# Tokens feature first from the host, the late chunk loaded later, VectorE scaling from PSUM

## The chip, the cores and the metric

The kernel runs on one core of one Trainium2 chip. The time is the device time in microseconds (us) of one execution; below it, "span" is the time from the first to the last instruction of a profiled execution. Engines: TensorE (PE, with its weight loads PEld), VectorE (DVE), ScalarE (ACT), GpSimd (POOL) and SyncE (SP), which here only issues DMAs.

## What is computed

A trunk of two layers over 1024 latent tokens and 256 context tokens, width 1024, in float32. Layer 0 is a chunked gMLP beside a bidirectional diagonal state space model (S5), layer 1 is grouped-query attention. The change lies wholly in the front of layer 0: modulation and row norm of the tokens, and the first products of `h` with `we_in`.

```python
def _ada(cond, w, b):
    m = jax.nn.silu(cond) @ w + b            # cond: c for latents, c_ctx for context
    return jnp.split(m, 3, axis=-1)          # shift, scale, gate

def _prologue(x, ctx, c, c_ctx, g, w_mod, b_mod):
    hx = _rms_norm(x, g) * (1 + sc[:, None]) + sh[:, None]
    hc = _rms_norm(ctx, g) * (1 + scc) + shc
    h = jnp.concatenate([hc, hx], axis=1)    # 1280 tokens x 1024 features

# layer 0
u, v, g_a, xs, g_b = jnp.split(h @ w_in, [...], axis=-1)
y_a = _chunk_gmlp(u, v, ...) * silu(g_a)     # layer norm of v, 128x128 mixing of tokens
y_b = _s5_bidir(xs, ...) * silu(g_b)         # scan over tokens, state operators from lam, dt, B, C
x = x + gt * (concat(y_a, y_b) @ w_out)
```

`_rms_norm` is `x * rsqrt(mean(x*x) + eps) * g`. The state operators of S5 (`exp` and `sin`/`cos` of `lam*dt`, powers up to 8, and their products with B and C) are computed in the kernel too.

## The kernel before

Tokens are cut into three chunks, `CHUNKS = [(0, 256), (256, 512), (768, 512)]`: the context, and two chunks of latents. Features are eight blocks of 128 (`KT`). Every large product is made of three TensorE products, of a rounded high part and a low part of each operand: `hi` and `h_lo` for the tokens (regions A and B), and the two halves of a weight slot for the weights. ScalarE rounds (`weights_round`, `h_round`), VectorE subtracts (`weights_rest`, `h_rest`). Weights come through a ring of three 2 MiB slots in an order written out by hand in `early` (L297); a slot is loaded again when the products of its last tenant are done.

The front, in order:

- SP (from L410) loads the column vectors, the five token pieces of 1 MiB each (context, then four of x, one token a row of 4 KB), modulation blocks 0 and 1, v(0), blocks 2 and 3 outside the ring, v(1), blocks 4 and 5, xs(0). ScalarE's queue (L651 to L657) loads the identity, `lam`, `log_dt`, and `braw`, `Cx` and `dT` (B, C and D of S5).
- ScalarE squares each token tile with a sum (L662), takes the root of all ten sums (L726), and scales the even tiles (L729); VectorE refines the root (`row_rstd`, L1024) and scales the odd tiles (L1112).
- TensorE makes modulation block m (`mods(m)`, 64 products of two rows) and turns its row into columns (`mod_cols`), and turns the scaled tokens feature first (`to_features(q)`, transposes into four PSUM banks). ScalarE (k = 0, 2, 3, 5, 6) and VectorE (k = 1, 4, 7) copy these out (`raw_evac`) into `hT0`.
- `half_evac(e)` on VectorE gathers scale and shift of feature half e. `h_round(e, q)` on ScalarE and `h_rest(e, q)` on VectorE make `hi` and `h_lo` of half e of chunk q. The first products of v need half 0 of chunk 0.
- v is made token by token (`v_part`): the first half of its columns for tiles 0 to 5 over k 0 to 3, then over k 4 to 7, then the second column half and the rest. Then come the 12 parts of xs (feature block x chunk; chunk 0 has 256 columns, the others 512). Between tiles and parts stand other jobs in the order of `after_v` and `after_xs` (L341, L343); TensorE and ScalarE both go by these two lists, each with its own part of a job.

Beside this, VectorE carries the parameters of S5: two exponentials (`exp_`, L1040), the sine, the parity of the quarter turns, a reciprocal, which releases `s_trig` (L1125). GpSimd waits for it (L540) and makes the cosine, the discretized lambda and its powers, some 60 small instructions, each waiting for the one before. VectorE waits for their end (L1151), then makes BB, the B operators (`build_bl(0)` to `(3)`) and the C operators (`build_cl(0)` and `(1)`, ended by a copy that releases `s_cl_ok`). The lists say who needs what:

```python
after_v = {1: [("mods", 4)], 2: [("cols", 4)], 5: [("mods", 5)], 6: [("cols", 5), ("xs", 0)], 7: [("bop", 0)], 8: [("bop", 4)],
           9: [("lags", 0)]}
after_xs = {0: [("xs", 1)], 2: [("bop", 8)], 4: [("ws", 0)], 5: [("lags", 1)], 6: [("gb", 0), ("bop", 12)], 7: [("vg", 0)],
            8: [("vg", 5)]}
```

`("xs", 1)` is ScalarE's rounding of xs(1). `("lags", half)` is on TensorE the lag products of S5 (`lags`, needs `s_cl_ok` half + 1), on ScalarE the copies of their result (`k_copies`), which VectorE's `k_diagonal(half)` waits for. `("bop", j)` are transposes of the B operators and their way out. SP stores the C operators with `cop_out(half)` (four DMAs, after `s_cl_ok`) and the lags with `kt_out(half)` (15 DMAs, after `k_diagonal`). On SP's queue stand, in this order: `cop_out(0)`, load of xs(1), `kt_out(0)`, load of gb(0), `cop_out(1)`, `kt_out(1)`, load of the B operators. When all xs parts are done, TensorE mixes v (L1798, ten tiles), and then multiplies by the B operators (L1814).

The helper lines of the rows: L1008 and L1011 are `tt` and `ts` of VectorE, L649 is `copy` of ScalarE, L1598 is `tr` of TensorE, L1613 is `mods`, L1732 to L1734 are `token_part`, L1743 to L1745 `feature_part`, L532 to L538 are GpSimd's small helpers, L403 is `ring_load`, L432 `cop_out`, L439 and L442 `kt_out`.

## Time and profile before

| | us |
|---|---|
| median of 3 runs | 1304.54 (1301.89 to 1306.85) |
| the profiled execution | 1301.15 |
| its span | 1299.3 |
| TensorE busy | 1223.0 (94%) |
| VectorE busy | 851.6 (66%) |
| ScalarE busy | 518.3 (40%) |
| GpSimd busy | 445.6 (34%) |

A share of busy time is an average over stages with different limits, and a busy TensorE may be waiting inside its pipeline. So the profile is read by stage: the timelines of the engines over the first 340 us, in which each group of instructions has its start, its length and, in brackets, how long its engine stood idle before it and who ended that. "DMA to landing" is the time from the start of the issue to the last byte.

### The profile page before, as it was taken

The page shows a single profiled execution, that of the slowest core. Times are in us where ns is not written, and L with a number is a line of the kernel's source. Part 1 is how long each engine was busy: PE and PEld are TensorE (multiplying, and loading weights), DVE is VectorE, ACT ScalarE, POOL GpSimd, SP SyncE. Part 2 cuts the span into 40 slices and gives each one's busy share as a digit, 9 for nine tenths or more (in the row PEclk, how much of TensorE's full clock was granted, in tenths as well). Part 3 has the DMA queues.
Part 4 walks back from the last instruction along what each step waited for, and adds up shares of the span by engine and source line. Part 5 has one row for each costly group of instructions (what it writes and reads, how often), then busy time and mean ns, then how long its engine had stood idle before and what let it go on. Part 6 is the DMA issues. An engine that isn't in the chain of part 4 may idle for free.

```text
span 1299.3 us, 21119 instructions
## 1 busy us (share of the span) xinstructions
PE 1223.0 (94%) x8508; PEld 1079.1 (83%) x8508; DVE 851.6 (66%) x1494; ACT 518.3 (40%) x956; POOL 445.6 (34%) x358
## 2 busy tenths in 40 slices
PE   1799989999999899999999999999999999999997
PEld 1789878888888848999999998877788888888997
DVE  6697956989925253136484899448877877776125
ACT  6632353320015331034524432146666666665012
POOL 0600000000000003332112212139999888988332
PEclk9899999999999999999999999999999999999999
DMA  9614677425422962103211112330000000000402
GB/s 347 241 66 130 153 209 247 148 81 203 162 90 85 324 231 56 64 33 116 70 44 34 33 66 81 111 100 9 9 17 9 17 9 17 17 9 9 162 28 103
DMA packets 87408, 127.99 MB, mean 99 GB/s; under 512 B 12912, under 2 KB 59376, under 8 KB 86512
## 3 DMA queue, kind: packets, MB, share of 16 engines
q1 hardware_dynamic: 77200, 110.81, 25.8%
q10 hardware_dynamic: 10112, 15.85, 3.5%
q8 instruction: 67, 1.10, 0.3%
q14 instruction: 29, 0.24, 0.1%
HBM read 95.71 MB, written 30.93 MB: 97 GB/s over the span
## 4 chain that ended last, share of the span: by engine, by line
PE 78%; DVE 11%; DMA 4%; ACT 3%; POOL 3%; issue 2%; SPq 0%; ACTq 0%; POOLq 0%; DVEq 0%
PE ps L1732 10%; PE ps L1734 10%; PE ps L1733 10%; PE ps L1743 5%; PE ps L1744 5%; PE ps L1745 5%; PE ps L1986 3%; DVE region_d L1008 3%; PE ps L2020 2%; PE ps L2021 2%; PE ps L2022 2%; PE ps L2006 2%; PE ps L2009 2%; PE ps L2008 2%; PE ps L2007 2%; PE ps L1598 2%
## 5 line engine op out<-in xcount | busy, mean ns | idle before, releaser
L1732 PE MATMUL ps<-w_hi,a_hi 128*128 128x256 f32 x896 | 256.6, 286 | 9.9 <-DVE b_lo L1109 6.3
L1733 PE MATMUL ps<-w_lo,a_hi 128*128 128x256 f32 x896 | 254.9, 284 | 0.0
L1734 PE MATMUL ps<-w_hi,c_lo 128*128 128x256 f32 x736 | 208.2, 283 | 0.0
L601 POOL TENSOR_TENSOR region_b<-region_b,region_d 128x256 f32<-128x256 f32 x40 | 29.7, 749 | 510.0 <-DVE region_d L1412 510.0
L1732 PEld LDWEIGHTS ps<-w_hi,a_hi 128*128 128x128 f32 x896 | 173.2, 193 | 12.2 <-issue 3.7
L1733 PEld LDWEIGHTS ps<-w_lo,a_hi 128*128 128x128 f32 x896 | 173.4, 194 | 0.0
L594 POOL TENSOR_TENSOR w_lo<-weight_ring,w_hi 128x2048 fp32r<-128x2048 f32 x16 | 74.0, 4625 | 199.3 <-ACT w_hi L649 199.3
L1734 PEld LDWEIGHTS ps<-w_hi,c_lo 128*128 128x128 f32 x736 | 141.2, 192 | 0.0
L1743 PE MATMUL ps<-a_hi,w_hi 128*128 128x512 f32 (+1 forms) x384 | 138.6, 361 | 1.4 <-ACT region_d L649 1.4
L1508 DVE TENSOR_REDUCE small<-ps 128x1 f32<-128x1280 f32 x64 | 95.2, 1487 | 65.1 <-PE ps L1986 65.1
L1744 PE MATMUL ps<-b_lo,w_hi 128*128 128x512 f32 (+1 forms) x384 | 136.6, 356 | 0.0
L1745 PE MATMUL ps<-a_hi,w_lo 128*128 128x512 f32 (+1 forms) x384 | 136.4, 355 | 0.0
L623 POOL TENSOR_TENSOR region_c<-region_c 128x512 f32<-128x512 f32 x80 | 113.6, 1420 | 27.2 <-ACT region_c L983 24.0
L623 POOL TENSOR_TENSOR region_c<-region_c,region_b 128x512 f32<-128x512 f32 x64 | 97.1, 1518 | 7.8 <-ACT region_b L983 1.6
L649 ACT ACTIVATE w_hi<-weight_ring 128x2048 fp32r<-128x2048 f32 x28 | 53.7, 1916 | 103.3 <-DMA weight_ring<-in_we_out 46.6
L1548 DVE TENSOR_TENSOR p_lo<-region_c,p_hi 128x512 fp32r<-128x512 f32 x64 | 85.0, 1329 | 4.3 <-ACT p_hi L649 4.2
L983 ACT ACTIVATE region_c<-ps 128x512 f32<-128x512 f32 x96 | 57.3, 597 | 76.3 <-PE ps L2009 76.2
L1743 PEld LDWEIGHTS ps<-a_hi,w_hi 128*128 128x128 f32 x384 | 73.2, 191 | 13.5 <-ACT region_d L649 1.6
L1745 PEld LDWEIGHTS ps<-a_hi,w_lo 128*128 128x128 f32 x384 | 73.1, 190 | 10.3
L1744 PEld LDWEIGHTS ps<-b_lo,w_hi 128*128 128x128 f32 x384 | 73.3, 191 | 9.5
L1008 DVE TENSOR_TENSOR region_d<-region_d 128x128 f32<-128x128 f32 (+1 forms) x178 | 72.2, 406 | 6.1
L1734 PE MATMUL ps<-w_hi,ot_lo 128*128 128x256 f32 x256 | 72.4, 283 | 0.0
(225 smaller groups left out, 2940.9 us busy)
## 6 DMA issues: line engine op xcount, KB each, us to landing
weight_ring<-in_w_mod SPq DMA_DIRECT2D x10, 2048.0 KB, 8.5
weight_ring<-in_we_in SPq DMA_DIRECT2D x10, 1024.0 KB, 6.0
weight_ring<-in_wo_in SPq DMA_DIRECT2D x10, 1024.0 KB, 5.2
weight_ring<-cop_t_scratch SPq DMA_DIRECT2D x4, 1536.0 KB, 7.9
region_a<-in_x SPq DMA_DIRECT2D x4, 1024.0 KB, 14.4
region_c<-in_w_mod SPq DMA_DIRECT2D x2, 2048.0 KB, 19.3
bop_scratch<-region_d ACTq DMA_DIRECT2D x16, 256.0 KB, 2.6
cop_t_scratch<-region_d SPq DMA_DIRECT2D x8, 512.0 KB, 7.4
```

The lines of the kernel that those rows point to most:

```text
L594: g.tensor_tensor(wl, slot_raw(u), wh.bitcast(F32), ALU.subtract).then_inc(s_w_lo, 1)
L623: g.tensor_tensor(psum_p[:, i % 2], PF[(m - 1) % NP] if t == 1 else psum_p[:, i % 2], PF[m % NP], ALU.add).then_inc(s_a_sum, 1)
L983: a.activation(PF[m % NP], ps[:, 3 + m % 2, :], ACT.Exp).then_inc(s_a_p, 1)
L1008: step(v.tensor_tensor(o, a, b, op))
L1508: v.tensor_reduce(smax[:, i % 2, h:h + 1], ps[:, 0:3, :].rearrange("p b n -> p (b n)")[:, 0:TOK], AX.X, ALU.max).then_inc(s_a_max, 1)
L1548: v.tensor_tensor(p_lo[:, (m - 1) % NP], PF[(m - 1) % NP], p_hi[:, (m - 1) % NP].bitcast(F32), ALU.subtract).then_inc(s_a_pld, 1)
L1732: te.matmul(o, th, wh[:, k], start=k == 0, stop=False)
L1733: te.matmul(o, th, wl[:, k], start=False, stop=False)
L1734: last = te.matmul(o, tl, wh[:, k], start=False, stop=k == last_k)
L1743: te.matmul(o, wh[:, k, fs], th, start=k == 0, stop=False)
L1744: te.matmul(o, wh[:, k, fs], tl, start=False, stop=False)
L1745: last = te.matmul(o, wl[:, k, fs], th, start=False, stop=k == KT - 1)
```

## The change

The host also lays out all 1280 tokens feature first (`xt`, 128 partitions x 8 blocks x 1280 tokens). The kernel loads this into `hT0` directly, in five DMAs: chunk 0, the two feature halves of chunk 1, and, behind block 2, the two of chunk 2. `braw` and `Cx` are loaded by SP behind block 3. TensorE's 80 transposes, the 24 copies and the ten row scalings go. In their place:

- ScalarE squares each piece into region A (128x2048), TensorE sums them over the features for each token with a column of ones, ScalarE takes the root, VectorE refines it (`token_rstd`), and TensorE spreads it over the partitions with transposes (`rstd_across`). For chunk 2, GpSimd first adds the eight blocks of squares in three steps, and TensorE needs four products.
- VectorE multiplies chunks 0 and 1 by that row straight from PSUM (`scale_tokens`, three instructions of 2048 elements). For chunk 2 ScalarE copies the row to SBUF (`rstd_rows`), and VectorE takes scale and rstd in one instruction, and shift and subtraction in another (`h_last`); ScalarE rounds with the shift (`h_round2`).
- The order on VectorE: `exp_(dt)`, `token_rstd(0)`, `(1)`, `scale_tokens`, sine, low part of v(0), `half_evac(0)`, `h_rest(0, 0)`, `(0, 1)`, low part of v(1), and only then `exp_(mg)`, parity and the reciprocal with `s_trig`; then `half_evac(1)`, `h_rest(1, 0)`, `(1, 1)`, `token_rstd(2)`, `h_last`.
- v starts with k 0 to 3 of both column halves for tiles 0 to 5. `mods(2)` moves behind the first of its tiles. `after_v` and `after_xs` are arranged anew, and `mod_evac(0, 6, 16, 24)` of VectorE moves behind the low part of xs(1), the low part of xs(0) ahead of `build_cl(0)`.

```diff
-        early = [(M[0], 0), (M[1], 1), (("v", 0), 2), (("v", 1), 0), (M[4], 1), (M[5], 1), (("xs", 0), 1), (("xs", 1), 0),
+        early = [(M[0], 0), (("v", 0), 2), (M[1], 1), (("v", 1), 0), (M[4], 1), (M[5], 1), (("xs", 0), 1), (("xs", 1), 0),
...
+        BCB = (2, 3, 7)
+        def sums(q):
+            t0, nt = CHUNKS[q]
+            return ps[:, 6, P:P + nt // P] if q == 2 else ps[:, q, 0:nt // P]
         VB = (4, 5, 0, 1, 2, 3, 4, 5, 4, 5)
         CB = (6, 7, 4, 5)
-        after_v = {1: [("mods", 4)], 2: [("cols", 4)], 5: [("mods", 5)], 6: [("cols", 5), ("xs", 0)], 7: [("bop", 0)], 8: [("bop", 4)],
-                   9: [("lags", 0)]}
-        after_xs = {0: [("xs", 1)], 2: [("bop", 8)], 4: [("ws", 0)], 5: [("lags", 1)], 6: [("gb", 0), ("bop", 12)], 7: [("vg", 0)],
-                    8: [("vg", 5)]}
+        after_v = {1: [("bc", 2)], 2: [("mods", 4)], 3: [("cols", 4)], 5: [("mods", 5)], 6: [("cols", 5)], 7: [("xs", 0), ("bop", 0)],
+                   9: [("bop", 4)]}
+        after_xs = {1: [("xs", 1)], 2: [("lags", 0)], 4: [("bop", 8)], 5: [("ws", 0)], 7: [("lags", 1)], 8: [("gb", 0), ("bop", 12)],
+                    9: [("vg", 0)], 10: [("vg", 5)]}
...
-            token_loads(X, ld_x)
-            ring_load(*M[0])
-            ring_load(*M[1])
-            ring_load("v", 0)
-            for m, done in ((2, s_ld_v), (3, s_ld_ws)):
+            xt = xt_in.rearrange("p (k t) -> p k t", t=TOK)
+            def feature_load(ks, q, done):
+                t0, nt = CHUNKS[q]
+                sp.dma_start(hT0[:, ks, t0:t0 + nt], xt[:, ks, t0:t0 + nt]).then_inc(done, 16)
+            def off_ring_load(m, done):
                 b = M[m][1]
                 sp.dma_start(off_ring[m].rearrange("p (k n) -> p k n", n=512),
                              w_mod[0][:, 512 * b:512 * b + 512].rearrange("(k p) n -> p k n", p=P)).then_inc(done, 16)
+            feature_load(slice(0, KT), 0, ld_x[0])
+            feature_load(slice(0, 4), 1, ld_x[1])
+            feature_load(slice(4, KT), 1, ld_x[2])
+            ring_load(*M[0])
+            ring_load("v", 0)
+            ring_load(*M[1])
             ring_load("v", 1)
+            off_ring_load(2, s_ld_v)
+            feature_load(slice(0, 4), 2, ld_x[3])
+            feature_load(slice(4, KT), 2, ld_x[4])
+            off_ring_load(3, s_ld_ws)
+            sp.dma_start(braw.rearrange("p r g h -> p (r g h)"), b_in).then_inc(s_ld_b, 16)
+            sp.dma_start(Cx.rearrange("p r g h -> p (r g h)"), c_in).then_inc(s_ld_b, 16)
...
+            pool.wait_ge(s_z, 3)
+            t0, nt = CHUNKS[2]
+            pool.wait_ge(s_sq, 5)
+            for i, m in enumerate((4, 2, 1)):
+                a, b = XQ[:, 0:m, t0:t0 + nt], XQ[:, m:2 * m, t0:t0 + nt]
+                g.tensor_tensor(a, a, b, ALU.add).then_inc(s_z, 1)
+                pool.wait_ge(s_z, 4 + i)
...
-            for t in range(TT):
-                act.wait_ge(ld_x[t // 2], 16)
-                squares(X[:, t], RB[:, 0:D], t, s_sq)
-            act.wait_ge(s_sq, TT)
-            act.wait_ge(s_consts, 2)
-            a.activation(rstd, ssq, ACT.Sqrt, bias=epsc, scale=1.0 / D).then_inc(s_rt0, 1)
...
+            def feature_squares(i, ks, q):
                 t0, nt = CHUNKS[q]
-                for k in ks:
-                    j = KT * q + k
-                    act.wait_ge(s_h_tr, j + 1)
-                    copy(hT0[:, k, t0:t0 + nt], ps[:, j % 4, 0:nt]).then_inc(s_h_eva, 1)
+                act.wait_ge(ld_x[i], 16)
+                a.activation(XQ[:, ks, t0:t0 + nt], hT0[:, ks, t0:t0 + nt], ACT.Square).then_inc(s_sq, 1)
+            def token_cols(q):
+                t0, nt = CHUNKS[q]
+                return slice(t0 // P, (t0 + nt) // P)
+            def token_root(q):
+                act.wait_ge(s_ss_mm, q + 1)
+                act.wait_ge(s_consts, 2)
+                a.activation(rstd[:, token_cols(q)], sums(q), ACT.Sqrt, bias=epsc, scale=1.0 / D).then_inc(s_rt, 1)
+            def rstd_copy(q):
+                t0, nt = CHUNKS[q]
+                act.wait_ge(s_bc_mm, q + 1)
+                copy(rstd_rows, ps[:, BCB[q], 0:nt]).then_inc(s_bc_ok, 1)
...
+            def h_round2():
+                t0, nt = CHUNKS[2]
+                for k in range(KT):
+                    act.wait_ge(s_z2, k + 1)
+                    a.activation(hi[:, k, t0:t0 + nt], hT0[:, k, t0:t0 + nt], ACT.Identity,
+                                 bias=modc[0][:, k, 0:1]).then_inc(s_h_hi, 1)
+            feature_squares(0, slice(0, KT), 0)
+            feature_squares(1, slice(0, 4), 1)
+            token_root(0)
+            feature_squares(2, slice(4, KT), 1)
+            token_root(1)
+            weights_round(("v", 0))
+            mod_row(0)
             mod_row(1)
-            raw_evac(1, (0, 2, 3, 5, 6))
-            weights_round(("v", 0))
-            act.wait_ge(s_h_tr, 16)
             h_round(0, 0)
+            h_round(0, 1)
+            weights_round(("v", 1))
             mod_row(2)
-            h_round(0, 1)
-            raw_evac(2, (0, 2, 3, 5, 6))
-            act.wait_ge(s_h_tr, 24)
+            feature_squares(3, slice(0, 4), 2)
+            feature_squares(4, slice(4, KT), 2)
             mod_row(3)
-            h_round(0, 2)
             h_round(1, 0)
             h_round(1, 1)
-            weights_round(("v", 1))
-            h_round(1, 2)
+            token_root(2)
+            rstd_copy(2)
+            h_round2()
...
+            def token_rstd(q):
+                t0, nt = CHUNKS[q]
+                c = slice(t0 // P, (t0 + nt) // P)
+                dve.wait_ge(s_rt, q + 1)
+                ts(msq[:, c], sums(q), 1.0 / D, ALU.mult, EPS, ALU.add)
+                step(v.reciprocal(rstd[:, c], rstd[:, c]))
+                tt(ssq[:, c], rstd[:, c], rstd[:, c], ALU.mult)
+                tt(ssq[:, c], ssq[:, c], msq[:, c], ALU.mult)
+                ts(ssq[:, c], ssq[:, c], -0.5, ALU.mult, 1.5, ALU.add)
+                v.tensor_tensor(rstd[:, c], rstd[:, c], ssq[:, c], ALU.mult).then_inc(s_rs0, 1)
             exp_(dt, ldt)
+            token_rstd(0)
+            token_rstd(1)
             tt(xe, lamr, dt, ALU.mult)
-            exp_(mg, xe)
             tt(th, lami, dt, ALU.mult)
-            ts(ki, th, 2.0 / math.pi, ALU.mult)
-            cp(kf, ki)
-            cp(rr, th)
+            def scale_tokens(ks, q, n):
+                t0, nt = CHUNKS[q]
+                dve.wait_ge(s_bc_mm, q + 1)
+                z = hT0[:, ks, t0:t0 + nt]
+                v.tensor_tensor(z, z, ps[:, BCB[q], 0:nt].unsqueeze(1).broadcast_to([P, n, nt]), ALU.mult).then_inc(s_z, 1)
+            scale_tokens(slice(0, KT), 0, KT)
+            scale_tokens(slice(0, 4), 1, 4)
+            scale_tokens(slice(4, KT), 1, 4)
...
+            def h_last(ks):
+                t0, nt = CHUNKS[2]
+                if ks[0] == 0:
+                    dve.wait_ge(s_bc_ok, 1)
+                for k in ks:
+                    z = hT0[:, k, t0:t0 + nt]
+                    v.scalar_tensor_tensor(out=z, in0=z, scalar=hA[0][:, k, 0:1], in1=rstd_rows,
+                                           op0=ALU.mult, op1=ALU.mult).then_inc(s_z2, 1)
+                for k in ks:
+                    dve.wait_ge(s_h_hi, 16 + k + 1)
+                    v.scalar_tensor_tensor(out=h_lo[:, k, t0:t0 + nt], in0=hT0[:, k, t0:t0 + nt], scalar=modc[0][:, k, 0:1],
+                                           in1=hi[:, k, t0:t0 + nt].bitcast(F32), op0=ALU.add, op1=ALU.subtract).then_inc(s_h_lod, 1)
+            weights_rest(("v", 0))
+            half_evac(0)
+            h_rest(0, 0)
+            h_rest(0, 1)
+            weights_rest(("v", 1))
+            exp_(mg, xe)
+            cp(kf, odd)
+            ts(ki, odd, 1.0, ALU.mult)
...
             half_evac(1)
-            h_rest(0, 2)
             h_rest(1, 0)
             h_rest(1, 1)
-            weights_rest(("v", 1))
-            h_rest(1, 2)
+            token_rstd(2)
+            h_last(range(4))
+            h_last(range(4, KT))
...
-            mod_evac(0, 6, 16, 24)
+            weights_rest(("xs", 0))
             build_cl(0)
...
             weights_rest(("xs", 1))
+            mod_evac(0, 6, 16, 24)
...
+            def token_sums(q, e):
+                t0, nt = CHUNKS[q]
+                for i in range(nt // P):
+                    for k in (range(KT) if e is None else range(4 * e, 4 * e + 4)):
+                        last = te.matmul(sums(q)[:, i:i + 1], XQ[:, k, t0 + P * i:t0 + P * i + P], onec, start=k == 0 and i == 0,
+                                         stop=k == KT - 1 and i == nt // P - 1)
+                return last
+            def rstd_across(q):
+                t0, nt = CHUNKS[q]
+                pe.wait_ge(s_rs0, q + 1)
+                for i in range(nt // P):
+                    t = t0 // P + i
+                    last = tr(ps[:, BCB[q], P * i:P * i + P], rstd[:, t:t + 1].broadcast_to([P, P]))
+                last.then_inc(s_bc_mm, 1)
+            pe.wait_ge(s_sq, 1)
+            token_sums(0, None).then_inc(s_ss_mm, 1)
+            pe.wait_ge(s_sq, 2)
+            token_sums(1, 0)
+            pe.wait_ge(s_sq, 3)
+            token_sums(1, 1).then_inc(s_ss_mm, 1)
+            rstd_across(0)
             mods(0)
+            rstd_across(1)
             mod_cols(0)
-            to_features(0, *x0)
             mods(1)
             mod_cols(1)
...
+            ws = [split_of(("v", 0))]
             for t in range(6):
                 if t == 2:
-                    to_features(2, *x0)
+                    mods(2)
+                    mod_cols(2)
+                for k in range(4):
+                    if t in (0, 2):
+                        pe.wait_ge(s_h_lod, k + 1 if t == 0 else k + 5)
+                    v_part(ws[0], t, 0, (k,))
+            ws.append(split_of(("v", 1)))
+            for t in range(6):
+                if t == 2:
                     mods(3)
+                if t == 3:
                     mod_cols(3)
-                if t in (0, 2):
-                    pe.wait_ge(s_h_lod, {0: 4, 2: 8}[t])
-                if t >= 2:
-                    h0_readers(18 + t)
-                v_part(ws, t, 0, range(4))
-            for t in range(6):
-                if t in (0, 2):
-                    pe.wait_ge(s_h_lod, {0: 16, 2: 20}[t])
-                v_part(ws, t, 0, range(4, KT))
-            ws = [ws, split_of(("v", 1))]
+                v_part(ws[1], t, 1, range(4))
+            t0, nt = CHUNKS[2]
+            pe.wait_ge(s_z, 6)
+            for i in range(nt // P):
+                last = te.matmul(sums(2)[:, i:i + 1], XQ[:, 0, t0 + P * i:t0 + P * i + P], onec, start=True, stop=True)
+            last.then_inc(s_ss_mm, 1)
             for t in range(TT):
-                if t == 6:
-                    pe.wait_ge(s_h_lod, 24)
+                if t in (0, 2, 6):
+                    pe.wait_ge(s_h_lod, {0: 12, 2: 16, 6: 24}[t])
                 if t >= 6:
                     pe.wait_ge(s_v_ev, t - 5 if t < 8 else t - 1)
-                    v_part(ws[0], t, 0)
-                v_part(ws[1], t, 1).then_inc(s_v_mm, 1)
+                ks = range(4 if t < 6 else 0, KT)
+                v_part(ws[0], t, 0, ks)
+                v_part(ws[1], t, 1, ks).then_inc(s_v_mm, 1)
                 between_tiles(after_v.get(t, ()))
```

## Rows read from the trace of the kernel before

**Rows 1.** TensorE's waits, 0 to 340 us: line, releaser, total, times, longest

```profile
PE ps L1613 <- DMA weight_ring<-in_w_mod: 27.2, 2, 26.8
```

**Rows 2.** Timeline of TensorE: start, length, line, operands, count, idle before it

```profile
26.84 3.60 PE L1613 MATMUL ps<-weight_ring,small 128*2 128x128 f32 x64 [26.84 <-DMA weight_ring<-in_w_mod]
...
48.99 0.55 PE L1732 MATMUL ps<-w_hi,a_hi 128*128 128x256 f32 x1 [3.12 <-DVE b_lo L1109]
...
164.73 0.28 PE L1685 MATMUL ps<-region_d 128*16 128x16 f32 x8 [1.65 <-DVE region_d L1182]
...
215.80 1.25 PE L1814 MATMUL ps<-region_c,weight_ring 128*128 128x160 f32 x8
```

**Rows 3.** Windows: stretch, length, busy by engine, granted clock, DMA, GB/s

```profile
46.00:48.00 2.00, 0.00 (x0) 0.00 (x0) 1.90 (x7) 2.00 (x4) 1.61 (x6) 0.50 1.08 357
```

**Rows 4.** Timeline of VectorE, 33 to 165 us

```profile
33.68 0.35 DVE L1125 RECIPROCAL shared<-shared 128x32 f32<-128x32 f32 x1
...
48.76 0.54 DVE L1011 TENSOR_SCALAR region_b<-region_b,small 128x512 f32<-128x512 f32 x1
...
49.95 0.54 DVE L1011 TENSOR_SCALAR region_b<-region_b,small 128x512 f32<-128x512 f32 x1
...
80.08 1.41 DVE L1008 TENSOR_TENSOR region_d<-region_d,shared 128x512 f32<-128x512 f32 x2
...
106.74 0.17 DVE L1142 TENSOR_TENSOR small<-ps,small 128x16 f32<-128x16 f32 x1 [6.76 <-PE ps L1598]
...
124.60 2.29 DVE L1038 TENSOR_TENSOR w_lo<-weight_ring,w_hi 128x2048 fp32r<-128x2048 f32 x1
...
164.50 0.17 DVE L1182 COPY region_d<-region_d 128x16 f32<-128x16 f32 x1
```

**Rows 5.** Timeline of ScalarE, 133 and 203 us

```profile
133.15 2.29 ACT L649 ACTIVATE region_d<-ps 16x448 f32<-16x448 f32 x4 [0.57 <-PE ps L1691]
...
203.46 0.60 ACT L649 ACTIVATE weight_ring<-ps 128x512 f32<-128x512 f32 x1 [4.84 <-PE ps L1745]
```

**Rows 6.** DMA issues at 3.9, 4.6, 130.8, 203.5: KB, us to landing

```profile
weight_ring<-in_w_mod SPq DMA_DIRECT2D x1, 2048.0 KB, 22.8
...
weight_ring<-in_w_mod SPq DMA_DIRECT2D x1, 2048.0 KB, 27.6
...
weight_ring<-in_we_in SPq DMA_DIRECT2D x1, 1024.0 KB, 10.0
...
weight_ring<-bop_scratch SPq DMA_DIRECT2D x1, 2048.0 KB, 9.1
```

**Rows 7.** Timeline of VectorE at 506 us, GpSimd busy from 504.89 to 509.5

```profile
506.57 0.42 DVE L1412 TENSOR_TENSOR region_d<-ps,shared 128x256 f32<-128x256 f32 x1 [2.46 <-PE ps L1734]
```

**Rows 8.** Groups by form, 0 to 340 us: busy us, mean ns, idle before

```profile
L649 ACT ACTIVATE w_hi<-weight_ring 128x2048 fp32r<-128x2048 f32 x9 | 17.2, 1912 | 8.1 <-DMA weight_ring<-in_we_in 7.3 <-ACT shared L812 0.8
...
L1008 DVE TENSOR_TENSOR shared<-shared 128x32 f32<-128x32 f32 x35 | 6.7, 192 | 1.2
```

**Rows 9.** Timeline of GpSimd, 26 to 60 us

```profile
34.12 0.22 POOL L535 TENSOR_SCALAR shared<-shared 128x32 f32<-128x32 f32 x1 [33.70 <-DVE shared L1125]
...
43.95 2.13 POOL L538 COPY shared<-shared 128x32 f32<-128x32 f32 x2
...
59.35 0.31 POOL L535 TENSOR_SCALAR lam<-shared 128x32 f32<-128x32 f32 x1
```

**Rows 10.** Timeline of GpSimd at 660 us

```profile
659.96 4.66 POOL L594 TENSOR_TENSOR w_lo<-weight_ring,w_hi 128x2048 fp32r<-128x2048 f32 x1 [22.56 <-ACT w_hi L649]
```

**Rows 11.** Timeline of VectorE at 660 us

```profile
660.18 4.92 DVE L1008 TENSOR_TENSOR region_d<-region_b,region_d 128x128 f32<-128x128 f32 x2
```

**Rows 12.** Timeline of SP, issues of DMAs, 124 to 197 us

```profile
124.59 6.17 SPq L432 DMA_DIRECT2D cop_t_scratch<-region_d  x4
...
182.31 1.87 SPq L439 DMA_DIRECT2D cop_t_scratch<-region_d  x2
...
195.47 1.56 SPq L442 DMA_DIRECT2D cop_t_scratch<-region_d  x1
```

118 lines of the change are left out of this document (43 added, 75 removed).

## The prediction, made before the change was run

> **What bounds the kernel now.** I read the waits of TensorE first, over the first 340 us, since every edit lies there. TensorE is idle for 27.2 us until the first modulation block has landed [rows 1]; its later waits there are 1 to 3 us each. Then I followed TensorE in order of time [rows 2]: the first modulation product runs at 26.84, the first product of v only at 48.99, and that wait ended with VectorE's low part of the tokens. The granted clock was then 0.50, the 1.2 GHz level, after an empty stretch [rows 3]. So the front is a chain: 5 MiB of tokens, modulation block 0, row norm, transposes, copies, rounding, first product.
>
> The second thing to see is that this chain isn't alone. VectorE carries a parameter chain, which from 80.08 builds the state operators and ends with the copy at 164.50 [rows 4]. TensorE's `lags(1)` starts 0.2 us later, at 164.73 [rows 2]. The last xs part is copied out from 203.46 [rows 5], and the products with the B operators begin at 215.80 [rows 2]. What follows shifts with those, as its loads are released by slots. What counts is therefore whether 215.80 moves, not whether 48.99 does.
>
> **The front: loads and the first product.** Block 0 was issued at 3.9 and landed 22.8 us later, at 26.7; block 1, issued at 4.6, landed 27.6 us later, at 32.2 [rows 6]: 2 MiB in 5.5 us, 2.7 us per MiB. Ahead of block 0 stand 5 MiB of tokens and 1 MiB of `braw` and `Cx`; the change leaves 3 MiB of tokens, so it lands at 26.7 - 3 x 2.7 = 18.6. SP then passes v(0), block 1, v(1), block 2, the late chunk, block 3, and b and c: block 1 lands at 26.7, the late chunk at 40.2, block 3 at 45.6, each before it is wanted. The token rows are 1 or 2 KB long instead of 4 KB; no row prices that here. I take 0, with 2 us as the upper end (an estimate, half of what one chunk takes in all).
>
> `mods(0)` took 3.60 us [rows 2]: 22.2. The transposes of rstd for chunk 1 wait behind it in TensorE's queue (0.5): 22.7. Scaling 2048 elements from PSUM isn't in the trace. Its ends are the 2.29 us of a 2048 element subtraction in SBUF [rows 4] and 8 x 0.42 = 3.4 from a 256 element product with a PSUM operand [rows 7]; I take the first, being of the same length. Two stand behind that wait: 27.3. Sine chain, 18 small ones at 0.19 + 0.03 us [rows 8]: 31.3. Low part of v(0), 2.3, and the modulation columns, 0.7: 34.3. First rounded tile 0.6 later, low parts 4 x 0.79 and 4 x 1.19 (1.19 is the distance of two starts in [rows 4], 0.79 the same for 256 elements): 42.8. TensorE starts v at about 35.7, 13 us before 48.99, and loses 80 transposes; 24 copies and ten row scalings go from ScalarE and VectorE. Alone this is a gain of 13 us or more.
>
> **What takes its place.** After 42.8 VectorE has the low part of v(1) (2.3), `exp_(mg)` (26 x 0.22 = 5.7) and the parity chain with the reciprocal (4.3): `s_trig` at 55.1, where before that reciprocal ran at 33.68 [rows 4]. GpSimd's parameter chain waits for it. It ran from 34.12 to 59.66, 25.5 us [rows 9], hidden then, as VectorE wanted it only at 80.08.
>
> Into the same stretch go GpSimd's three sums of the late chunk's squares. ScalarE comes to these squares after `h_round(0, 1)`, rounding v(1) (1.9 [rows 8]) and a modulation row, so they end at about 46. On GpSimd 2048 elements cost 4.62 us [rows 10], the next two sums half and a quarter or so of that: it works from 46 to 54.4. What that does to VectorE can be seen later in the trace: GpSimd's 2048 element instruction starts at 659.96 and ends at 664.6 [rows 10], and two VectorE products of 128 elements from 660.18 take 4.92 us [rows 11], where two of 512 take 1.41 [rows 4]. VectorE was held until GpSimd was done. The small products in `exp_(mg)` have two SBUF operands, as those have. Of 8.4 us VectorE gets some 1.6 between the sums: 6.8 lost, `s_trig` at 61.9. Ends: 0 (nothing held) and 8.4.
>
> The Trainium skill says the same in SBUF — State Buffer, section "Who interferes with whom": a VectorE instruction with two SBUF inputs and a GpSimd instruction that reads SBUF share a port pair, and whichever is first keeps it to its end. By that rule the loss is the whole of GpSimd's time less the gaps; the trace agrees, with the 4.92 us above.
>
> The parameter chain then runs on GpSimd beside a busy VectorE. Two of its 128x32 copies took 2.13 us from 43.95, where the first and last instructions of the chain take 0.22 and 0.31 [rows 9]; VectorE's 2048 element subtraction ran meanwhile. That hold goes (-1.7), and the chain now stands beside some 24 us of VectorE's 512 element instructions, not 8 (+3; ends 0 and 12, a wait of 0.2 for each of some 60). I take 27: done at 88.9. VectorE itself finishes the late chunk (16 at 0.7 [rows 4] after its wait for rstd) at about 85. So the operators start at 88.9, not at 80.1.
>
> **From there to the B products.** Before, 84.4 us lay between 80.1 and 164.5 [rows 4]. One part of them goes: the 6.8 us of waiting for the columns of block 5, which ended at 106.74 [rows 4], since `mod_evac` moves behind the work that it held up. One comes in. `s_cl_ok` reaches 1 at 88.9 + 37.7 + 2.3 = 128.9 (37.7 is 124.6 - 80.1 - 6.8 [rows 4]; the low part of xs(0) now stands ahead). SP issues the four stores in 6.2 us [rows 12], then xs(1), which lands 10.0 after its issue [rows 6]: 145.1. ScalarE waits for that behind xs part 1 (before: part 0). Queued behind this wait are its evacuation of part 2 (0.6), which TensorE's part 4 needs, and `k_copies(0)` (4.6, two groups like that at 133.15 [rows 5]), which VectorE's `k_diagonal(0)` needs: 145.1 + 1.9 + 0.6 + 4.6 = 152.2. VectorE could be there at 148.5, so 3.7 are lost. `s_cl_ok` reaches 2 at 88.9 + 84.4 - 6.8 + 3.7 = 170.2, against 164.5.
>
> TensorE reaches `lags(1)` at about 170 too: v starts 13 us earlier, but stands 7 before its second halves (`half_evac(1)` is behind `s_trig` on VectorE), 4 at `cols(4)` behind ScalarE's late rounding, and 4 before part 4. What helps is the order: `lags(1)` now stands behind part 7, not part 5, so of the 31.0 us from its end (172.5) to 203.5 a short part (2.9) and a long one (5.4) are gone. 170.4 + 7.8 + 22.7 = 200.9, a gain of 2.6.
>
> One more pin. `k_diagonal(1)` stands behind the low part of gb(0), whose rounding now follows part 8, not 6. Part 8 ends at 185.1; evacuation, rounding, subtraction and diagonal take 5.6: 190.7. SP's stores behind it take 14.7 (182.31 to 197.03 [rows 12]), and the operator load behind those 9.1 [rows 6]: 214.5. Before, it had 6.4 us to spare. TensorE would be ready at 200.9 + 12.3 = 213.2. The later decides: 214.5 for 215.8, a gain of 1.3. The edits of semaphores, of `dT` and of the final gain's landing cost nothing: they wait for the same transfers, long landed, as do the loads of b and c, which are wanted only at 88.9.
>
> The profiled execution took 1301.15 us with a span of 1299.3. The span becomes 1298.0 and the execution 1299.9. The median of the three runs lies 3.4 above the profiled one, which gives 1303.3.
>
> **The rivals.**
> 1. GpSimd's sums hold nothing. For it: a product of VectorE that reads PSUM takes 0.42 us in the middle of GpSimd's 2048 element instruction [rows 7]. Against: [rows 11], with SBUF operands. Then `s_trig` is at 55.1, the operators start 6.8 earlier, and the whole gains 8.1: 1296.
> 2. The parameter chain isn't the bound at all, and xs(1) lands in time. TensorE's own gain is left, 13 us: 1291. Against it: the wait at 106.74 is the only one in VectorE's 84.4 us.
> 3. Slower. GpSimd's chain is starved: some 60 instructions, each dependent on the one before, beside VectorE's of 0.54 and 0.7 us. Each us that it ends after 88.9 is one us of `s_cl_ok` 2. Half as long again as before (38 us) makes 11 later, 10 slower than before: 1314. It decides from 34.8 us on, where the whole is 0.5% slower. For it: 43.95 in [rows 9]; against: only two instructions are hit like that.
> 4. The change doesn't do what it says: the short rows load so slowly that block 0 lands where it did. The sum then gives some 5 us more than before: 1309.
>
> **How the numbers follow.** Forecast 0.43, with its own range 1298 to 1309 (the hold some us less, or the ends of the chain). Rival 1 0.26, rival 2 0.07, rival 3 0.18, rival 4 0.06. 0.5% is 6.5 us, about what a measurement of this kernel can tell from no change. Faster: nine tenths of rival 1, rival 2, a little of the forecast, 0.32. Slower: most of rival 3, a third of rival 4, a little of the forecast, 0.21. Within: 0.47. The range takes in rival 1, the lower half of rival 3 and rival 4: 1291 to 1312.
>
> **What would show it.** First product of v near 36. GpSimd's three sums near 46, with small products of VectorE of over 1 us under them; without those rival 1 holds. The reciprocal ahead of `s_trig` near 62, GpSimd's last small instruction near 89, VectorE's first operator product right behind it; above 97 it is rival 3. `lags(1)` near 170 with VectorE as its releaser, and the B products near 214.5 behind the load of the operators. If `lags(1)` starts without a wait, the chain isn't the bound and the forecast is wrong.

## The result and the profile after

The changed kernel takes 1320.18 us, the median of four runs (1317.25 to 1321.18), against 1305.05 for the kernel before beside it (1301.89 to 1306.85): a ratio of 1.0115, with a 95% interval of 1.0089 to 1.0141. It is slower by 15 us, where 1303.3 was forecast and 1312 was the upper end of the range. The profiled execution took 1319.8 us with a span of 1318.0 (before: 1299.3), so 18.7 us more.

Waits of TensorE over the first 360 us, the answer to [rows 1], the longest total first; columns: engine, line, releaser, us in total, times, longest.

```profile
PE ps L1818 <- DVE b_lo L1166: 15.2, 2, 10.3
PE ps L1726 <- ACT region_a L754: 10.2, 1, 10.2
PE ps L1668 <- ACT mod_row L679: 5.3, 3, 4.5
PE ps L1891 <- ACT weight_ring L679: 3.6, 1, 3.6
```

At the start TensorE now waits 10.2 us, for ScalarE's squares, where it waited 27.2 us before; yet the first product of v comes as late as ever. TensorE's timeline (start, length, engine and line, tile, shapes, count, and in brackets the idle time before it and its releaser), beside [rows 2]:

```profile
10.16 20.61 PE L1726 MATMUL ps<-small,region_a 128*128 128x1 f32 x96 [10.16 <-ACT region_a L754]
31.23 3.38 PE L1683 MATMUL ps<-weight_ring,small 128*2 128x128 f32 x64
34.54 0.65 PE L1668 MATMUL ps<-ident,small 128*128 128x128 f32 x4
48.19 0.55 PE L1818 MATMUL ps<-w_hi,a_hi 128*128 128x256 f32 x1 [10.26 <-DVE b_lo L1166]
...
234.51 9.15 PE L1907 MATMUL ps<-region_c,weight_ring 128*128 128x160 f32 x64
```

From 10.2 to 30.8 TensorE does nothing but the token sums: 48 products of one column each, in 96 records (two to a product) of 215 ns apiece. The modulation product starts behind them at 31.2 (its block had landed by 19.0, as e1 shows below), and rstd of chunk 1 goes across at 34.5. ScalarE and VectorE stand and wait for those sums; ScalarE's root and VectorE's refinement:

```profile
30.81 0.26 ACT L764 ACTIVATE small<-ps,small 128x4 f32<-128x4 f32 x1 [11.59 <-PE ps L1726]
...
31.11 0.16 DVE L1054 TENSOR_SCALAR small<-ps 128x4 f32<-128x4 f32 x1 [12.43 <-ACT small L764]
```

VectorE from the scaling to the second set of operators, beside [rows 4]:

```profile
35.22 4.49 DVE L1126 TENSOR_TENSOR region_b<-region_b,ps 128x2048 f32<-128x2048 f32 x2 [0.30 <-PE ps L1668]
60.55 4.50 DVE L1051 TENSOR_TENSOR shared<-shared 128x32 f32<-128x32 f32 x1
65.08 2.40 DVE L1054 TENSOR_SCALAR shared<-shared 128x32 f32<-128x32 f32 x1
67.73 1.15 DVE L1054 TENSOR_SCALAR shared<-shared 128x32 f32<-128x32 f32 x1
...
74.39 0.35 DVE L1202 RECIPROCAL shared<-shared 128x32 f32<-128x32 f32 x1
89.09 2.84 DVE L1175 SCALAR_TENSOR_TENSOR region_b<-region_b,small,region_d 128x512 f32<-128x512 f32 x4 [3.98 <-ACT region_d L679]
...
104.41 1.42 DVE L1051 TENSOR_TENSOR region_d<-region_d,shared 128x512 f32<-128x512 f32 x2 [2.38 <-POOL lam L557]
144.91 0.17 DVE L1253 COPY region_d<-region_d 128x16 f32<-128x16 f32 x1
...
185.17 0.17 DVE L1253 COPY region_d<-region_d 128x16 f32<-128x16 f32 x1
```

The scaling from PSUM is as priced, 2.24 us for each of the two. Then three small instructions last 4.50, 2.40 and 1.15 us, the reciprocal ahead of `s_trig` comes at 74.4, and the operators start at 104.4, released by GpSimd. Beside them GpSimd's three sums and two groups of its parameter chain:

```profile
60.33 8.52 POOL L567 TENSOR_TENSOR region_a<-region_a 128x2048 f32<-128x2048 f32 x3 [59.91 <-ACT region_a L754]
78.21 5.13 POOL L554 TENSOR_TENSOR shared<-shared 128x32 f32<-128x32 f32 x10
...
99.51 3.66 POOL L560 COPY shared<-shared 64x512 f32<-64x512 f32 x4
```

From the operators on the lag shrinks, and from the B products on everything is shifted as a block: it is 24.3 us at their start (104.4 for 80.1), 20.7 at the second `s_cl_ok` (185.2 for 164.5), 18.7 at the B products (234.5 for 215.8) and 18.7 at the end.

The same milestones for all kernels, from the profiled execution of each (us); the ratio is to the kernel before, of timed runs. A span is of one execution and can lie some us off the median (e4's was 2.8 above that of its ten). Two of these kernels leave sums out: e1 on TensorE and e3 on GpSimd.

| kernel | ratio (95%) | first v | reciprocal | operators | `s_cl_ok` 2 | B products | span |
|---|---|---|---|---|---|---|---|
| before | 1 | 49.0 | 33.7 | 80.1 | 164.5 | 215.8 | 1299.3 |
| changed | 1.0115 (1.0089-1.0141) | 48.2 | 74.4 | 104.4 | 185.2 | 234.5 | 1318.0 |
| e1 sums cut | 1.0056 (1.0038-1.0074) | 36.7 | 62.7 | 92.6 | 172.7 | 222.8 | 1311.0 |
| e2 v(1) late | 1.0129 (1.0109-1.0149) | 47.9 | 74.0 | 104.0 | 184.7 | 233.6 | 1316.4 |
| e3 GpSimd's sums cut | 1.0063 (1.0043-1.0083) | 48.4 | 67.1 | 97.3 | 177.2 | 225.3 | 1308.8 |
| e4 chain early | 1.0020 (1.0008-1.0031) | 44.3 | 28.8 | 87.4 | 172.2 | 221.7 | 1307.2 |
| e5 | 1.0013 (0.9999-1.0027) | 44.2 | 29.2 | 88.0 | 172.1 | 222.3 | 1304.7 |
| e6 | 1.0013 (1.0000-1.0026) | 36.3 | 56.8 | 90.2 | 174.3 | 219.3 | 1302.3 |
| e7 old lists | 1.0085 (1.0061-1.0109) | 47.7 | 73.7 | 103.8 | 181.5 | 229.4 | 1313.6 |
| e8 filler | 1.0102 (1.0071-1.0134) | 48.0 | 74.2 | 104.3 | 184.5 | 233.8 | 1318.5 |
| e9 = e6 + orders | 0.9965 (0.9950-0.9980) | 35.9 | 51.8 | 85.1 | 163.6 | 215.5 | 1299.6 |
| e10 = e5 + orders | 0.9951 (0.9932-0.9970) | 44.8 | 28.9 | 85.2 | 162.9 | 210.8 | 1295.4 |
| e11 = e4 + orders | 0.9972 (0.9958-0.9986) | 43.8 | 28.9 | 87.6 | 165.5 | 214.6 | 1297.2 |

### The profile page after: what moved, and what is told of

Read it like the earlier page. It is cut to its first block, busy times and chain, and to the rows that moved or that the text cites. A ratio compares the mean times of both kernels' runs of the same rounds, so it can differ in the third digit from the quotient of the medians.

```text
span 1318.0 us, 21151 instructions
## 1 busy us (share of the span) xinstructions
PE 1243.9 (94%) x8542; PEld 1099.6 (83%) x8542; DVE 855.2 (65%) x1496; ACT 504.1 (38%) x924; POOL 468.4 (36%) x361
## 4 chain that ended last, share of the span: by engine, by line
PE 74%; DVE 9%; DMA 7%; POOL 4%; ACT 3%; issue 2%; SPq 1%; ACTq 0%; POOLq 0%; DVEq 0%
PE ps L1818 10%; PE ps L1820 10%; PE ps L1819 10%; PE ps L1829 4%; PE ps L1830 4%; PE ps L1831 4%; DVE region_d L1051 3%; POOL region_c L653 3%; PE ps L2079 3%; PE ps L2113 2%; PE ps L2114 2%; PE ps L2115 2%; PE ps L2144 2%; PE ps L2145 2%; PE ps L2146 2%; PE ps L2099 2%
## 5 line engine op out<-in xcount | busy, mean ns | idle before, releaser
L1818 PE MATMUL ps<-w_hi,a_hi 128*128 128x256 f32 x896 | 260.2, 290 | 18.9 <-DVE b_lo L1166 15.2
L1819 PE MATMUL ps<-w_lo,a_hi 128*128 128x256 f32 x896 | 257.7, 288 | 0.0
L1818 PEld LDWEIGHTS ps<-w_hi,a_hi 128*128 128x128 f32 x896 | 176.3, 197 | 21.2 <-issue 12.1
L1819 PEld LDWEIGHTS ps<-w_lo,a_hi 128*128 128x128 f32 x896 | 176.5, 197 | 0.0
L653 POOL TENSOR_TENSOR region_c<-region_c 128x512 f32<-128x512 f32 x80 | 125.9, 1573 | 18.1 <-ACT region_c L1026 13.8
L2113 PE MATMUL ps<-p_hi,v_hi 128*128 128x512 f32 x160 | 66.0, 413 | 7.0 <-DVE p_lo L1618 3.1
## 6 DMA issues: line engine op xcount, KB each, us to landing
region_b<-in_xt SPq DMA_DIRECT2D x5, 1024.0 KB, 11.6
```

The source lines that it names most:

```text
L653: g.tensor_tensor(psum_p[:, i % 2], PF[(m - 1) % NP] if t == 1 else psum_p[:, i % 2], PF[m % NP], ALU.add).then_inc(s_a_sum, 1)
L1818: te.matmul(o, th, wh[:, k], start=first and k == 0, stop=False)
L1819: te.matmul(o, th, wl[:, k], start=False, stop=False)
L2113: te.matmul(o, Vh[:, t, hd], p_hi[:, m % NP], start=t == 0, stop=False)
```

## The experiments

Five theories: (1) TensorE's token sums stand in everything's way; (2) SyncE's queue does, which waits for slot 0 with v(1) ahead of the late chunk; (3) GpSimd's sums hold VectorE; (4) VectorE's parameter chain stands too late; (5) the rearranged lists cost time by themselves.

**e1: fewer token sums.**

```diff
-                    for k in (range(KT) if e is None else range(4 * e, 4 * e + 4)):
+                    for k in ((0, 7) if e is None else (7 * e,)):
```

> The changed kernel, but TensorE adds up only features 0 to 127 and 896 to 1023 of the squares of chunks 0 and 1 (12 products of one column instead of 48), so the row norms of those tokens are left too small a sum. Theory 1 (the 20.6 us of token sums on TensorE push back everything behind them): the second root is ready near 21 instead of 30.8, rstd of chunk 1 then waits for the first modulation product (block 0 lands at about 20), the first v product comes near 38 instead of 48.2, the reciprocal ahead of s_trig near 64 instead of 74.4, the operators near 94 instead of 104.4, and the kernel is about 10 us faster than the changed one: some 1310. Theory 2 (the order of SyncE's queue, late chunk behind v(1)) and theory 3 (GpSimd's sums hold VectorE) and theory 4 (place of the parameter chain) alone: the first product comes earlier, but the operators stay at 104 and the time at 1318 to 1320.

Measured: operators 11.8 us earlier, B products 11.7, kernel 1311.55 us. TensorE now comes to the modulation product as its block lands:

```profile
16.16 1.87 PE L1726 MATMUL ps<-small,region_a 128*128 128x1 f32 x8 [1.50 <-ACT region_a L754]
19.01 3.60 PE L1683 MATMUL ps<-weight_ring,small 128*2 128x128 f32 x64 [0.45 <-DMA weight_ring<-in_w_mod]
...
36.65 0.55 PE L1818 MATMUL ps<-w_hi,a_hi 128*128 128x256 f32 x1 [4.87 <-DVE b_lo L1166]
...
92.64 1.42 DVE L1051 TENSOR_TENSOR region_d<-region_d,shared 128x512 f32<-128x512 f32 x2 [4.24 <-POOL lam L557]
```

The first v product at 36.65 is where the prediction had it (35.7). Theory 1 holds in place and size. The end of the profiled execution gains 7.0 us, 4.7 less than the B products. The two loads of the B operators took SyncE 15.3 us to issue instead of 12.1, TensorE waited 2.29 us for the second instead of 0.76, and the 64 products behind that wait took 10.63 us instead of 8.96. That is 3.2 of the 4.7; the rest isn't traced.

**e2: v(1) behind the late chunk.**

```diff
-            ring_load("v", 1)
             off_ring_load(2, s_ld_v)
             feature_load(slice(0, 4), 2, ld_x[3])
             feature_load(slice(4, KT), 2, ld_x[4])
             off_ring_load(3, s_ld_ws)
+            ring_load("v", 1)
```

> The changed kernel with the load of v(1), which waits for slot 0 until the first modulation product is done, moved behind block 2, the late chunk and block 3 in SyncE's queue. Theory 2 (that wait stops the loads and with it the late chunk's path): block 2 and the late chunk are issued near 16 instead of 35, the squares of the late chunk and GpSimd's sums come some 3 us earlier, and the kernel gains up to 5 us. Theory 1 (token sums) and theory 4 (chain): the late chunk's squares stand behind the rounding of v(1) and a modulation row on ScalarE anyway, the reciprocal stays within 1 us of 74.4, and the time within 2 us of 1320.

The reciprocal moved by 0.4 us, the B products by 0.9, and the ratio is no better than the changed kernel's. SyncE stands still for 19 us ahead of its issue of v(1) in the changed kernel:

```profile
34.67 0.37 SPq L410 DMA_DIRECT2D weight_ring<-in_we_in  x1
```

That costs nothing here, and theory 2 falls.

**e3: GpSimd's sums over 8 tokens.**

```diff
-                a, b = XQ[:, 0:m, t0:t0 + nt], XQ[:, m:2 * m, t0:t0 + nt]
+                a, b = XQ[:, 0:m, t0:t0 + 8], XQ[:, m:2 * m, t0:t0 + 8]
```

> The changed kernel, but GpSimd adds up the late chunk's squares for only 8 of its 512 tokens, the rest is left out. Theory 3 (GpSimd's sums hold VectorE's small products for 7.5 us ahead of s_trig): the reciprocal near 67 instead of 74.4, the operators 7.5 us earlier if GpSimd's chain is what they wait for; VectorE's own queue ended at 102.0 in the changed kernel, 2.4 before the chain, and gets shorter by the same 7.5; so 7 us faster, some 1313. If the small products had other causes for their 4.50 and 2.40 us, nothing moves. Theory 1 alone would give less than 1 us.

```profile
67.13 0.35 DVE L1202 RECIPROCAL shared<-shared 128x32 f32<-128x32 f32 x1
...
97.25 1.42 DVE L1051 TENSOR_TENSOR region_d<-region_d,shared 128x512 f32<-128x512 f32 x2 [5.84 <-POOL lam L557]
```

7.3 us off the reciprocal, 7.2 off the operators. The three long small instructions are gone with the sums, so theory 3 holds too. The wait for GpSimd ahead of the operators grew from 2.38 to 5.84: VectorE would have been ready at 91.4, and GpSimd's chain alone sets the time.

**e4: the parameter chain in VectorE's idle time.** Lines in parentheses stand for code that isn't shown.

```diff
             exp_(dt, ldt)
-            token_rstd(0)
-            token_rstd(1)
             tt(xe, lamr, dt, ALU.mult)
             tt(th, lami, dt, ALU.mult)
+            exp_(mg, xe)
+            (sine, parity, reciprocal with s_trig)
+            token_rstd(0)
+            token_rstd(1)
...
             param_ops.append(n[0])
+            (GpSimd's three sums, moved here from ahead of its chain)
```

> The changed kernel with the whole parameter chain of VectorE (second exponential, sine, parity, reciprocal: 14 us) moved into its idle time from 15.2 to 31.1, ahead of the row norms, and GpSimd's parameter chain ahead of its three sums. Nothing is left out. Theory 4 (the parameter chain placed late on VectorE is what the operators wait for): s_trig near 30, GpSimd's chain done near 60, the operators start when VectorE has finished the late chunk, near 90 instead of 104.4; 12 us faster or more, some 1307. Theory 1 in its strong form (the token sums delay all, wherever the chain stands): only the 4 us of the sine leave VectorE's path behind the scaling, and the gain is 4 us or less.

```profile
28.78 0.35 DVE L1145 RECIPROCAL shared<-shared 128x32 f32<-128x32 f32 x1
...
64.64 0.18 DVE L1164 TENSOR_TENSOR small<-ps,small 128x16 f32<-128x16 f32 x1 [8.87 <-PE ps L1668]
...
87.40 1.41 DVE L1051 TENSOR_TENSOR region_d<-region_d,shared 128x512 f32<-128x512 f32 x2
```

The token sums still take 20.6 us, but now VectorE works under them instead of waiting. The operators start at 87.4 and without a wait. The kernel takes 1306.19 us, about 1% less than the changed one. The strong form of theory 1 falls: the sums cost so much only because the chain that the operators need stood behind them. e4 also takes the parameter chain out from behind GpSimd's sums, the delay of e3, so its 17.0 us at the operators aren't e1's 11.8 alone. With GpSimd's chain done at 56.8, the bound in e4 is VectorE's own queue.

**e7: the old order of the side work.** `after_v` and `after_xs` as before, with the norms of the late chunk still behind tile 1.

```diff
-        after_v = {1: [("bc", 2)], 2: [("mods", 4)], 3: [("cols", 4)], 5: [("mods", 5)], 6: [("cols", 5)], 7: [("xs", 0), ("bop", 0)],
-                   9: [("bop", 4)]}
+        after_v = {1: [("bc", 2), ("mods", 4)], 2: [("cols", 4)], 5: [("mods", 5)], 6: [("cols", 5), ("xs", 0)], 7: [("bop", 0)],
+                   8: [("bop", 4)], 9: [("lags", 0)]}
...
```

> The changed kernel with the order of TensorE's and ScalarE's side work as it was before: modulation products 4 and 5 one tile earlier in v, xs(0)'s and xs(1)'s rounding, both lags, gb(0) and the value norm one or two tiles earlier. Theory 5 (this part of the change costs time by itself): 3 us or more faster than 1320. Theory 1 with theory 4: from the start of the operators on, the changed kernel loses nothing against before (130.1 us from there to the B products, 135.7 before), so the old lists give nothing or cost up to 5 us, since lags(1) then stands ahead of parts that could run while the second operators are built: 1320 to 1325.

The B products come 5.2 us earlier, and I had expected none or a loss. VectorE's waits behind the operators in the changed kernel (the low part of xs(0), `k_diagonal(0)`, the low part of gb(0)), and then `s_cl_ok` 2 and the low part of gb(0) in e7:

```profile
125.28 2.29 DVE L1081 TENSOR_TENSOR w_lo<-weight_ring,w_hi 128x2048 fp32r<-128x2048 f32 x1 [0.96 <-ACT w_hi L679]
...
166.97 0.41 DVE L1051 TENSOR_TENSOR region_d<-ident,small 16x256 f32<-16x256 f32 x1 [2.18 <-ACT region_d L679]
...
203.59 2.29 DVE L1081 TENSOR_TENSOR w_lo<-weight_ring,w_hi 128x2048 fp32r<-128x2048 f32 x1 [9.40 <-ACT w_hi L679]
```

```profile
181.48 0.17 DVE L1253 COPY region_d<-region_d 128x16 f32<-128x16 f32 x1
...
192.80 2.29 DVE L1081 TENSOR_TENSOR w_lo<-weight_ring,w_hi 128x2048 fp32r<-128x2048 f32 x1 [2.31 <-ACT w_hi L679]
```

From the operators to `s_cl_ok` 2 it takes 77.6 us instead of 80.8: the wait of 2.18 at 166.97 for ScalarE's `k_copies` and one of 0.96 at the low part of xs(0) are gone. Another 0.6 us was there at the operators already. The last 1.5 us come behind `s_cl_ok` 2. TensorE's busy time between `lags(1)` and the causal mixing, changed kernel and then e7 (columns: window, length, PE busy and count, granted clock, DMA share, GB/s):

```profile
185.40:221.60 36.20, 29.19 (x305) 0.95 0.67 200
```

```profile
181.60:216.40 34.80, 34.69 (x351) 1.00 0.88 250
```

In the new order 7.8 us of work have indeed left this stretch (before: 36.99 busy of 39.30), but 7.0 us of gaps have come in, at 193.96, 212.29 and 221.58. The first and the last of them in TensorE's timeline, and what ScalarE did ahead of the last:

```profile
193.96 0.50 PE L1830 MATMUL ps<-b_lo,w_hi 128*128 128x512 f32 x1 [2.36 <-issue]
...
221.58 12.91 PE L1891 MATMUL ps<-shared,region_c 128*128 128x128 f32 x80 [3.56 <-ACT weight_ring L679]
```

```profile
216.15 3.63 ACT L745 ACTIVATE region_c<-region_c,small 128x512 f32<-128x512 f32 x5
...
220.84 0.60 ACT L679 ACTIVATE weight_ring<-ps 128x512 f32<-128x512 f32 x1 [1.07 <-DMA xs_scratch<-weight_ring]
```

The gaps of 1.09 and 3.56 us belong to the new order: all eight kernels with the new lists have both (1.0 to 2.4, and 2.1 to 4.0), and the five with the old lists have 0.78 in place of the second and none of the first. ScalarE copies out the last xs part only at 220.84, behind the second half of the value norm (`("vg", 5)`), which the new lists put behind part 10, and a wait of 1.07. And the gap costs more than its length: for 3.4 us behind it the granted clock reads 0.56, and the mixing takes 12.9 us where it took 11.6 before and in e7.

The gap of 2.36 us is another matter. "Issue" means that the profile shows nothing that TensorE waited for; the granted clock then reads 0.52 for 3.4 us. Nine of the thirteen kernels have such a gap (1.6 to 2.6 us) in or just behind `lags(1)`, the kernel before (1.71 at 170.95) and e9 with the old lists among them. e6, e7, e10 and e11 have none there (e6 has one of 3.15 earlier, at 148.46). From `s_cl_ok` 2 to the B products, in us:

| | with this gap | without it |
|---|---|---|
| old lists | 51.3 (before), 51.9 (e9) | 47.9 (e7), 47.9 (e10), 49.1 (e11) |
| new lists | 49.3 (changed), 48.1 to 50.3 (e1 to e5, e8) | 45.0 (e6) |

Like with like, the new order is some 2 to 3 us shorter here, and a kernel with the gap is some 3 to 5 us longer. So the 1.5 us that e7 wins behind `s_cl_ok` 2 come with the missing gap, and not from the old order. By the time alone theory 5 holds: 4.7 us between the medians, though the intervals of the two ratios overlap. What the old order itself gains is seen only ahead of `s_cl_ok` 2, 3.1 us. Why the gap comes in some kernels and not in others, no run shows.

**e8: TensorE busy ahead of the sums.**

```diff
+            for i in range(16):
+                te.matmul(ps[:, 5, 0:P], ident[:], ident[:], start=True, stop=True)
             pe.wait_ge(s_sq, 1)
```

> The changed kernel with 16 products of 128x128 on the identity on TensorE ahead of the token sums, in its idle time between 5 and 10 us. Nothing is left out. The 96 records of the token sums take 215 ns each from 10.2 to 30.8; the eight of the late chunk, at 73, take 119 ns. If TensorE is slow there because it stood idle before, the sums take nearer to 11.4 us, theory 1 then gives up to 9 us: some 1311. If the filler is not enough, or the pace of these products has another cause, the sums stay at 20.6 us and the time at 1320.

```profile
11.77:14.00 2.23, 2.23 (x23) 1.00 1.05 386
14.00:16.20 2.20, 2.20 (x13) 0.54 1.05 387
16.20:19.00 2.80, 2.80 (x14) 0.50 1.05 377
```

The first 23 records of the sums run at 97 ns each; then the granted clock falls to 0.50, the 1.2 GHz level, although TensorE is busy without a gap, and the other 73 take 16.1 us, 220 ns each. The sums take 18.3 instead of 20.6 us and end 0.7 us earlier: next to nothing gained. The 215 ns of the changed kernel are within 3% of the pace at 0.50, so its sums ran at the pace of the low clock, and a filler ahead of them doesn't keep the clock up.

**e5 and e6: the fixes together.** e5 is e4 with the order of e2, the fourth modulation product in the first pass of v, and the late chunk's squares added on VectorE. e6 gives the 33 instructions of the two polynomials to GpSimd instead and lets VectorE add up chunk 1's squares before TensorE sums them (8 products for 32):

```diff
-                    for k in (range(KT) if e is None else range(4 * e, 4 * e + 4)):
+                    for k in (range(KT) if e is None else (4 * e,)):
...
```

> The run with the early parameter chain (e4), and in addition: block 2, the late chunk and block 3 ahead of v(1) in SyncE's queue, the fourth modulation product in the first pass over v (behind tile 3, its column transposes behind tile 4) instead of the second, and the late chunk's squares added up on VectorE instead of GpSimd. Nothing is left out. In e4 VectorE stood idle for 8.87 us until the columns of the fourth modulation block were there, and the operators began at 87.4 without a wait, so VectorE's own queue set it. If that is the bound, the wait goes, three sums (about 4.1 us) come into its place, and the operators begin near 82, the kernel comes 5 us below e4: some 1301. If the bound has by then gone over to TensorE or to the loads, the operators begin earlier but the B products do not, and the time stays at 1306.

> As e5, but the parameter chain is shared out: the two polynomials (33 small instructions) go to GpSimd, idle until then, the rest stays on VectorE behind the low part of v(1); and VectorE adds up the squares of chunk 1 in pairs of features first (two groups of 1.9 us), so that TensorE needs 8 products of one column for it instead of 32. Nothing is left out. Theory 1 (token sums on TensorE) and theory 4 (chain): TensorE's sums end near 22 instead of 30.8, the first v product comes near 36 instead of 44 to 48, s_trig near 50, GpSimd's chain ends near 79, the operators begin near 80, the kernel ends near 1297, below the kernel before. If GpSimd is slower beside VectorE than its 29.5 us, its chain is the last to arrive and the time is above e5's.

Both missed: the operators start at 88.0 and 90.2, not at 82 and 80, and the times are 1306.49 and 1305.43 us, no better than e4's. VectorE's waits, e5 and then e6:

```profile
77.42 2.74 DVE L1183 SCALAR_TENSOR_TENSOR region_b<-region_b,small,region_d 128x512 f32<-128x512 f32 x4 [5.45 <-ACT region_d L671]
```

```profile
49.61 2.29 DVE L1096 TENSOR_TENSOR w_lo<-weight_ring,w_hi 128x2048 fp32r<-128x2048 f32 x1 [6.40 <-ACT w_hi L694]
90.15 1.42 DVE L1066 TENSOR_TENSOR region_d<-region_d,shared 128x512 f32<-128x512 f32 x2 [0.78 <-POOL lam L558]
```

In e5 the wait for the modulation columns (8.87 in e4) is replaced by one of 5.45 for the norms of the late chunk, which TensorE sends across only behind two tiles of v. In e6 v(1), now behind block 3 in SyncE's queue, makes VectorE wait 6.4 us for its rounding, and GpSimd's chain takes 32.8 us and ends last.

**e9, e10, e11: with three orders put right.** The old lists (e7), the norms behind tile 0, and v(1) ahead of the fourth modulation block (the last one in e9 and e10). The new `after_v`; `after_xs` is as before:

```diff
...
+        after_v = {0: [("bc", 2)], 1: [("mods", 4)], 2: [("cols", 4)], 5: [("mods", 5)], 6: [("cols", 5), ("xs", 0)],
+                   7: [("bop", 0)], 8: [("bop", 4)], 9: [("lags", 0)]}
...
```

> The run e6 with three orders changed: the side work of TensorE and ScalarE stands as in the kernel before (e7 took 5.2 us off the B products with that alone), the norms of the late chunk are sent across behind tile 0 of v instead of tile 1 (VectorE waited 3.94 us for them), and v(1) is loaded ahead of the fourth modulation block (ScalarE waited 8.22 us for it). Nothing is left out. If the gains of the steps add up, the B products begin near 219.3 - 5 - 3 = 211 and the kernel ends some 5 us below before: 1299. If GpSimd's chain (it ended at 89.7 in e6) is what the operators wait for, only the lists count: 1301.

> The run e5 with the same three orders changed. VectorE waited 5.45 us for the norms of the late chunk, and GpSimd's chain was long done. The B products near 222.3 - 5 - 3 = 214, and the kernel 2 us or more below before, some 1301; where the norms come no earlier (TensorE reaches them only behind its own queue), 1303.

> The smallest set of order changes: the run e4 (parameter chain of VectorE ahead of the row norms, GpSimd's chain ahead of its sums) with the side work's order of the kernel before, and the late chunk's norms sent across behind tile 0. Nothing is left out. If e4 (14 us off the changed kernel) and e7 (5) are separate costs and add up, the B products begin near 216.5 and the time is 1301.5; if they are the same cost seen twice, it stays at e4's 1306.

e10 is the fastest, 1297.33 us, 0.5% below before and 1.6% below the changed kernel; e11, which only moves work and changes nothing else, gets 1299.6. The gains of e4 (14.0) and e7 (4.7) add up, and e11 gains 1.9 us more, having a third edit, the norms behind tile 0. From the operators to `s_cl_ok` 2, e4, e5 and e6 took 84.8, 84.0 and 84.2 us, and e11, e10 and e9 take 77.9, 77.7 and 78.4. e10 and e11 also lack the gap without a releaser, which the kernel before has; from `s_cl_ok` 2 to the B products e10 takes 47.9 us for 51.3, so 3.4 of its lead of 5.0 us over the kernel before at the B products come with that, and aren't shown to be the work of any edit. e10 came out 4 us below its expected 1301, e11 2 below, and e9 between its two values. e9 has the first v product at 35.9 and is still no faster than e10: VectorE waits 5.33 us for GpSimd's chain ahead of the operators. Its start of the operators, and then e10's with its B products:

```profile
85.14 1.42 DVE L1066 TENSOR_TENSOR region_d<-region_d,shared 128x512 f32<-128x512 f32 x2 [5.33 <-POOL lam L558]
```

```profile
85.23 1.41 DVE L1043 TENSOR_TENSOR region_d<-region_d,shared 128x512 f32<-128x512 f32 x2
...
210.80 18.43 PE L1909 MATMUL ps<-region_c,weight_ring 128*128 128x160 f32 x128
```

## Why the prediction was wrong

The view of the kernel was right: the time is set by when the operators start and what lies between them and the B products, not by the first v product. The forecast put the B products at 214.5; they came at 234.5. The 20.0 us missed have three places: 12.5, 3.0 and 5.0, less 0.5 that the stretch from the operators to `s_cl_ok` 2 came out shorter. One row of the kernel before bears on the first, eight TensorE records with a 128x128 stationary operand:

```profile
31.10 1.58 PE L1598 MATMUL ps<-ident,region_a 128*128 128x128 f32 x8
```

- **12.5 us: a term that isn't in the sum.** "`mods(0)` took 3.60 us: 22.2. The transposes of rstd for chunk 1 wait behind it: 22.7." Measured 35.2. The forecast lists the transposes that TensorE loses and of what it gains prices only those of rstd (0.5); the 48 one-column products of `token_sums` stand in the diff, ahead of `mods(0)` in the same queue, and cost 20.61. The trace of before has no such product, so it had to be bounded. At the pace of `mods(0)` in [rows 2], 3.60 us for 64 records, 96 records come to 5.4 us, all but hidden under the wait for block 0. But their stationary operand is 128x128 where that of `mods(0)` is 128x2, and the trace of before has records with such an operand right behind `mods(0)`, at 198 ns each (the row above). At that pace 96 records come to 19.0 us, near the 20.61 measured. All later marks of the forecast are 12.5 late by this alone: first v 48.2 for 35.7, reciprocal 74.4 for 61.9.
- **3.0 us: GpSimd's chain.** Priced at 27, it took 29.5. Its single instructions are slower: ten products from 78.21 take 5.13 us, where the same ten took 3.22 before. That is the mechanism of rival 3, well short of the 34.8 from which that rival decides. No run takes VectorE's work away from beside the chain, so that VectorE is the cause is argued. The rest is the step from the reciprocal to its first instruction.
- **5.0 us: the lists.** "What helps is the order" was the step that failed: the new order was to shorten the way from `s_cl_ok` 2 to the B products by 7.0 us, from 51.3 to 44.3, and did so by 2.0, to 49.3. The gain was counted from the work that leaves the stretch after `lags(1)` (8.3 forecast, 7.8 measured) as if TensorE would stay as busy as before. But the new order brought the gaps of 1.09 and 3.56 us (0.78 before), and the mixing behind them took 1.3 us longer. The gap without a releaser isn't part of this, for the kernel before has it too; e6, without it, shows that the new order is worth 2.9 us against e7 and e10. The loads were no better: the forecast had the operator load decide at 214.5, with TensorE ready at 213.2. The first of these loads, issued at 222.92, took 11.5 us instead of 9.1 and landed at 234.4, and TensorE was ready at 234.5.

What held: the scaling from PSUM (2.3 forecast, 2.24 measured); the hold of VectorE by GpSimd's sums (6.8 forecast, 7.3 by e3), against rival 1; the sums themselves (8.4 and 8.5, though [rows 10] shows 4.66 for the first, not 4.62); the wait for block 5's columns, gone; 81.3 us from the operators to `s_cl_ok` 2 (80.8), with the loss at `k_copies` seen (3.7 forecast, 3.1 measured with the low part of xs(0)); `lags(1)` released by VectorE, though at 185.4; and that what lies behind the B products only shifts (1083.5 us from them to the end in both kernels). Rival 4 didn't occur: e1 shows block 0 landed at 19.0, forecast 18.6. (Its time of 1309 doesn't come out of the forecast's terms: 8.1 us late, less the gain of 1.3, is 6.8 above before, 1311.) The wait of SyncE for slot 0 was overlooked in the forecast's order of loads and, by e2, without effect. Rival 2, that the parameter chain isn't the bound, falls by e3, where the operators moved by 7.2 us with TensorE's front unchanged, and the B products moved with it (9.2). One mark was ill chosen: "above 97 it is rival 3". The operators came at 104.4, and it wasn't rival 3, for the chain started late instead of running long; its start, at 74.9, tells the two apart.

The sign was wrong because two gains were set against the later start of the parameter chain, and neither came as priced. The parameter chain, moved behind the front, was to come 28.2 us later than before (33.7 to 61.9); the 13 us gained in the front were already in that figure, and they didn't come: it came 40.7 us later (33.7 to 74.4). Its end had 20.4 us to spare before (59.7 [rows 9] for 80.1), and it ran 4.0 longer: 40.7 + 4.0 - 20.4 = 24.3, the lag of the operators, for which 8.8 was forecast. The way from the operators to the B products was then to win back 10.1 us and won 5.6. Without either of the two large misses it would still be slower: by 18.7 - 12.5 = 6.2 us with the sums at no cost, by 18.7 - 5.0 = 13.7 with the lists as priced.

## What to carry over

- Before the rows of a profile are added up, list every instruction that the diff adds in each queue, in its order, and bound the ones that the trace doesn't show by the nearest rows on either side (here 5.4 and 19.0 us); the missing term, 12.5 us, was larger than any uncertainty that was weighed.
- Work moved out of an early idle stretch comes late by everything that it is moved behind, not by its own length; where the change makes an engine wait, that wait is the place for such work (e4).
- Work that leaves a stretch is a gain only where its engine stays busy: read the gaps, not the sum. And look for the same gap in the other kernels before it is put down to an edit: the one of 2.36 us came and went with either order.

## What the hardware showed

- A product of one column with a full 128x128 stationary operand costs two records of 215 ns at the start of the kernel and of 119 ns at 73 us. The granted clock (behind the counts) reads 1.00 in both places; e8 shows it drop to 0.50 there once TensorE has worked ahead. At the start of this program that column didn't tell the pace. The row of the products at 73 us, and then the windows of both (columns as above):

```profile
73.34 0.95 PE L1857 MATMUL ps<-small,region_a 128*128 128x1 f32 x8
```

```profile
20.00:31.00 11.00, 11.00 (x53) 1.00 0.64 229
...
73.00:75.00 2.00, 1.29 (x13) 1.00 0.00 0
```

- VectorE's small products weren't the only ones that GpSimd held: a scalar multiplication with a single tensor operand took 2.40 and 1.15 us under its sums, and 0.18 without. The Trainium skill allows for this in SBUF — State Buffer, section "Who interferes with whom", which counts `tensor_scalar` among the instructions that can take the port pair shared with GpSimd when their operands meet the conditions of a two-port mode; the trace agrees, with these two rows.
- GpSimd's chain of about 60 small instructions took 25.5 us before, 27.6 in e4, 29.5 in the changed kernel, 31.2 in e5 and 32.8 in e6, all on the same data. VectorE's busy share beside it doesn't order them: 62, 85, 74, 87 and 82%. The chain also costs VectorE: in e4 four subtractions of 512 elements took 0.83 to 0.98 us beside GpSimd's instructions of 128 to 512 elements (47.5 to 53.2), and 0.69 in the changed kernel from 50.9 on, with GpSimd idle.
